# Three low halves of the first two experts' weights on GpSimd, and the next experts' loads reordered

## The chip, the cores and the metric

The kernel runs on one core of a Trainium2 chip. A core has five engines that run at the same time and meet only through semaphores: TensorE (PE) multiplies matrices, VectorE (DVE), ScalarE (ACT) and GpSimd (POOL) work on elements, and SyncE (SP) issues transfers. Sixteen DMA engines move data between the main memory and the on-chip memory SBUF; PE writes to PSUM. The metric is the device time of one execution in microseconds (us), less is better.

## The reference, cut to what matters

One layer of a diffusion backbone over 640 tokens (128 of a prompt, 512 of a latent grid), model width 1024. After attention, convolution, output projection and LayerNorm comes a mixture of 16 experts. Each token picks one group of four experts and two experts in it:

```
g_idx = top_k(softmax(t @ wg + bg), 1);  e_idx = top_k(softmax(logits of that group), 2)
hid = t @ w_exp_in[e]            # 1024 x 512 for each expert
a, up = split(hid)
y   = (silu(a) * up * gate) @ w_exp_out[e]     # 256 x 1024
x   = layer_norm(ALPHA * x + gf * sum over the two experts of y)
```

All data are fp32.

## The kernel before, in words

**Precision.** Every fp32 matrix is split into a high part, rounded to the type fp32r (by ACT, a copy), and a low part, the rest (a subtraction by DVE). A product is three matmuls: high x high, high x low, low x high (lines 1756 to 1758). So each weight half that arrives in `raw` needs an ACT copy to `w_hi` and then a subtraction `w_lo = raw - w_hi` before PE may use it, and its home in `raw` is free for the next load when `w_lo` is there.

**Names.** The input weights of expert e come in two halves of 1 MB, h = 0 and 1. The prediction writes in(e,h) for the load of such a half (`expert_in`, line 514), out(e) for the load of the output weights (`expert_out`, line 526), w_hi(e,h) for the ACT copy (`expert_whi`, line 953) and half (e,h) or low half (e,h) for the subtraction (`expert_wlo`, line 1424; for (0,1) before the change `first_wlo_quarter`, line 1433). There are two homes for input weights and two for output weights; expert e uses home e mod 2. `olo` (line 1499) is the subtraction for the output weights, `act_lo` (line 1521) that of the activations.

**Stages.** The attention ends at about 280 us. Then, for five tiles of 128 tokens in turn, PE computes the output projection, DVE the LayerNorm (lines 1440 to 1497), the modulated rows h2, and, some tiles behind, the choice of experts from the router's logits (`choose`, line 1381) and the token's place in the expert's list with one-hot comparisons (`put`, line 1409). POOL stores each tile of h2 to main memory (line 651), from where each expert's rows are gathered by an indirect DMA (line 657). The rows of expert 0 aren't gathered from memory: PE picks them with one-hot products out of SBUF (`gather_first`, line 2077), the last of them when the last tile's places are known. Then the expert loop begins: for each expert an up projection in two halves (line 2152), transposes of the next expert's rows (line 2138), and the down projection of the expert before (line 2170).

**What sets the order.** Each engine's instructions stand in the program in a fixed order, and semaphores hold them. On DVE the tail of the last tile is followed by the choices and places of the last two tiles (lines 1526 to 1529), the low halves of expert 0, the list of places (line 1540), the low halves of expert 1, and the loop (line 1647). On SP the loads stand in one queue; each waits until its home is free, and one that waits holds all behind it. `s_wlo` counts the low halves with h = 0, `s_wlp` those with h = 1. in(1,1) and out(0) also wait for the last tile's h2, because their homes hold data of the LayerNorm until then. POOL has nothing to do beside DMAs in this stretch: the stores of h2, then, once the list is ready, the gathers and the stores of expert rows.

Of the kernel before, what the change touches and what calls it, by code (L numbers as in the profile page):

```python
# [5 lines left out]
def build(nc, ins, outs):  # L6


    fp32 = mybir.dt.float32
# [3 lines left out]
    ALU = mybir.AluOpType  # L13
# [10 lines left out]
    NT = TOK // P  # L24
# [10 lines left out]
    NE = ins["w_expert_in"].shape[1]  # L35
# [3 lines left out]
    CH = 512  # L39
# [33 lines left out]
    with ctx:  # L73
        def sb(name, shape, dt=fp32):
            return ctx.enter_context(nc.sbuf_tensor(name, shape, dt))

        def sem(name):
            return ctx.enter_context(nc.semaphore(name))
# [4 lines left out]
        w_hi = sb("w_hi", [P, 2, KD * CH], fp32r)  # L83
        w_lo = sb("w_lo", [P, 2, KD * CH], fp32r)
        raw = sb("raw", [P, 2, KD * CH])
# [30 lines left out]
        def dap(t, offset, pattern):  # L116
            return bass.AP(tensor=t.tensor, offset=offset, ap=pattern)
# [125 lines left out]
        E0 = 2 * NW  # L243
# [22 lines left out]
        s_whi = sem("w_hi_ready")  # L266
        s_wlo = sem("w_lo_ready")
        s_wlp = sem("expert_w_lo_second_half_ready")
        s_whp = sem("expert_w_hi_second_half_ready")
# [121 lines left out]
        def raw_slot(b):  # L391
            return raw[:, b, :].rearrange("p (k n) -> p k n", k=KD)
# [38 lines left out]
        def out_rows(t):  # L431
            return outs["y_prompt"][0] if t == NT - 1 else outs["y_sample"][0][t * P:(t + 1) * P, :]
# [3 lines left out]
        def _(sp):  # L436
# [77 lines left out]
            def expert_in(e, h):  # L514
                slot = e % 2
                if h == 0 or e < 2:
                    sp.wait_ge(s_wlo, e + E0 - 1)
                else:
                    sp.wait_ge(s_wlp, e - 1)
                if e == 1:  # L520

                    sp.wait_ge(s_h2, 1 if h == 0 else H2)
                src = we_in[e].rearrange("(k p) n -> p k n" if e == 0 else "(p k) n -> p k n", p=P)
                sp.dma_start(raw_slot(slot)[:, 4 * h:4 * h + 4, :], src[:, 4 * h:4 * h + 4, :]).then_inc(s_raw[slot][h], 16)

            def expert_out(e):
                slot = e % 2
                if e < 2:

                    sp.wait_ge(s_h2, H2)  # L530
                    sp.wait_ge(s_h2t, NT)
                    sp.wait_ge(s_h2s[2 * e], 16)
                    if e == 1:
                        sp.wait_ge(s_h2s[1], 16)
                        sp.wait_ge(s_hgt, 1)
                else:
                    sp.wait_ge(s_olo, e - 1)
                sp.dma_start(raw_o[:, slot, :].rearrange("p (k n) -> p k n", k=2),
                             we_out[e].rearrange("(p k) n -> p k n", p=P)).then_inc(s_rawo[slot], 16)
# [3 lines left out]
            for t in T_ORDER[:-1]:  # L543
                sp.dma_start(out_rows(t), dap(ins["ln2_b"], 0, [[0, P], [1, D]])).then_inc(s_pre, 16)
            expert_in(1, 0)
            expert_in(1, 1)
            expert_out(0)
            expert_in(2, 0)
            for e in range(2, NE + 2):

                if 2 < e < NE:
                    expert_in(e, 0)
                if e >= 4:
                    expert_out(e - 2)
                if e < NE:
                    expert_in(e, 1)
                if e == 2:
                    expert_out(1)

            sp.wait_ge(s_wlo, E0 + NE - 1)  # L560
            sp.wait_ge(s_wlp, NE - 1)
# [31 lines left out]
        def _(pool):  # L593
# [36 lines left out]
            def load_bias(g, a, last_use):  # L630

                if g >= 1:
                    pool.wait_ge(s_nm, 2 * (NB * (g - 1) + last_use) + 2)
                for side in range(2):
                    src = dap(bias_dram, (2 * g + side) * CB * 3 * TW + a * TW,
                              [[SPAN, ROWS], [3 * TW, CB], [1, LOC]])
                    pool.dma_start(bias_s[:, side, a, :], src).then_inc(s_bias[a], 16)  # L637
# [6 lines left out]
            for g in range(HP):  # L644
                load_bias(g, 2, 0)
                load_bias(g, 1, 2)
                load_bias(g, 0, 3)
            for n, t in enumerate(T_ORDER):

                pool.wait_ge(s_h2, n + 1 if n < NT - 1 else H2)  # L650
                pool.dma_start(h2_dram[t * P:(t + 1) * P, :].rearrange("p (k c) -> p k c", k=KD), h2_held[n]).then_inc(s_h2s[n], 16)
            pool.wait_ge(s_lc, 1)
            for n in range(NT):
                pool.wait_ge(s_h2s[n], 16)
# [56 lines left out]
        def _(act):  # L711
# [205 lines left out]
            def h2_copy(n):  # L917
                act.wait_ge(s_h2t, n + 1)
                if n >= 1:
                    act.wait_ge(s_lg, n)  # L920
                else:
                    act.wait_ge(s_mlo, HP + 1)
                for i in range(2):
                    if n == NT - 1:
                        act.wait_ge(s_h2t, NT + i)
                    nc.scalar.activation(h2_T[:, 4 * i:4 * i + 4, :], PS[:, 4 + i, :].rearrange("p (k t) -> p k t", k=4),
                                         ACT.Copy).then_inc(s_h2c, 1)

            def logits_copy(n):

                act.wait_ge(s_lp, n + 1)
                nc.scalar.activation(group_logits, PS[:, 4, 0:P], ACT.Copy).then_inc(s_lcp, 1)

            def root(n):

                act.wait_ge(s_var, n + 1)
                nc.scalar.activation(std[:, n % 2:n % 2 + 1], mv[:, n % 2, 1:2], ACT.Sqrt, bias=eps).then_inc(s_std, 1)
# [15 lines left out]
            def expert_whi(e, h):  # L953

                b = e % 2
                if e == 0:
                    act.wait_ge(s_mo0, 1)
                elif e == 1:
                    act.wait_ge(s_mo, NT)
                else:  # L960
                    act.wait_ge(s_hid, e - 1)
                act.wait_ge(s_raw[b][h], 16 * (len(LOADS[b]) + e // 2 + 1))
                half = slice(h * 4 * CH, (h + 1) * 4 * CH)
                nc.scalar.activation(w_hi[:, b, half], raw[:, b, half], ACT.Copy).then_inc((s_whi, s_whp)[h], 1)  # L964
# [41 lines left out]
                nc.scalar.activation(y_sb[:, 1, CH:D], PS[:, 3, :], ACT.Copy).then_inc(s_ya, 1)  # L1006

            expert_whi(0, 0)
            h2_copy(NT - 2)
            root(NT - 1)  # L1010
            logits_copy(NT - 2)
            expert_whi(0, 1)
            h2_copy(NT - 1)
            logits_copy(NT - 1)

            expert_whi(1, 0)
            expert_whi(1, 1)
            for h in range(2):
                if h == 0:
# [39 lines left out]
            with act.If(more > 0):  # L1059
# [3 lines left out]
                with act.Fori(0, more) as i:  # L1063

                    e = act.value_load(over_i[0:1, bass.ds(i + 1, 1)], min_val=0, max_val=NE - 1)
# [67 lines left out]
        def _(dve):  # L1133
# [8 lines left out]
            V = nc.vector  # L1142
# [281 lines left out]
            def expert_wlo(e, b, h):  # L1424
                if h == 0:
                    dve.wait_ge(s_whi, e + E0 + 1)
                else:
                    dve.wait_ge(s_whp, e + 1)
                half = slice(h * 4 * CH, (h + 1) * 4 * CH)
                V.tensor_tensor(w_lo[:, b, half], raw[:, b, half], w_hi[:, b, half].bitcast(fp32),  # L1430
                                ALU.subtract).then_inc((s_wlo, s_wlp)[h], 1)

            def first_wlo_quarter(k):

                dve.wait_ge(s_whp, 1)
                quarter = slice(k * CH, (k + 2) * CH)
                return V.tensor_tensor(w_lo[:, 0, quarter], raw[:, 0, quarter], w_hi[:, 0, quarter].bitcast(fp32), ALU.subtract)

            link(V.memset(uni[:, 5120:5200], 0.0))
            for n, t in enumerate(T_ORDER):  # L1440
# [58 lines left out]
            def expert_olo(e, b):  # L1499
                dve.wait_ge(s_ohi, e + 1)  # L1500
                oh, ol = {NE - 1: wo_last, NE - 2: wo_near}.get(e, (wo_hi, wo_lo)) if isinstance(e, int) else (wo_hi, wo_lo)
                V.tensor_tensor(ol, raw_o[:, b, :].rearrange("p (k n) -> p k n", k=2), oh.bitcast(fp32),  # L1502
                                ALU.subtract).then_inc(s_olo, 1)

            def gathered_lo(c, b):
                dve.wait_ge(s_ghi, c)
                V.tensor_tensor(hgT_lo[:, b, :, :], PS[:, 2:4, :].rearrange("p a (k t) -> p (a k) t", k=4),
                                hgT_hi[:, b, :, :].bitcast(fp32), ALU.subtract).then_inc(s_glo, 1)
# [24 lines left out]
            d12 = rs[:, 160:160 + NT]  # L1533
            link(V.tensor_tensor(gexp, logits[:, :, 0:NG], g_top[:, :, 0:1].to_broadcast([P, NT, NG]), ALU.subtract))
            V.tensor_tensor(d12, e_top[:, :, 1], e_top[:, :, 0], ALU.subtract).then_inc(s_d12, 1)
            expert_wlo(0, 0, 0)
            first_wlo_quarter(4)
            dve.wait_ge(s_ls, NT)
            second = list_t[:, 0:NE]
            link(V.tensor_scalar(second, PS[:, 7, 0:NE], PAGE - AWAY, -float(PAGE), ALU.is_ge, ALU.mult))  # L1540
# [11 lines left out]
                V.tensor_scalar(list_last[:, h:h + 1], PS[:, 7, NE - 1:NE], 2.0, 2.0 * AWAY + h, ALU.mult, ALU.add)  # L1552
            V.tensor_scalar(list_d[:, 0:NE], PS[:, 7, 0:NE], AWAY, None, ALU.add).then_inc(s_lc, 1)
            dve.wait_ge(s_gi, 1)
            first_wlo_quarter(6).then_inc(s_wlp, 1)
            expert_olo(0, 0)
            silu_times_up(0, 0)
            act_lo_sub(0, 0)
            gathered_lo(1, 1)
            expert_wlo(1, 1, 0)  # L1560
            expert_wlo(1, 1, 1)

            def chunk_count():

# [741 lines left out]
```

## Time and profile before

| | |
|---|---|
| median of three runs | 566.56 us |
| lowest and highest run | 565.86 and 571.65 us |
| the profiled execution: its span, first to last instruction | 567.2 us |
| PE busy | 510.6 us, 90% |
| DVE busy | 443.0 us, 78% |
| ACT busy | 272.9 us, 48% |
| POOL busy | 106.2 us, 19% |
| main memory, over the span | 257 GB/s |

The profile is that of one execution. It has no time of its own beside its span, which is 0.6 us above the median of the runs. Instructions are told by engine, source line and operation; "idle before" is how long the engine stood before an instruction, with what released it behind the arrow. The ends of matmuls are modelled, so their durations overlap: a row of 0.39 us stands for about 0.23 us of PE's time.

### The profile page before, as it was taken

The page shows a single profiled execution, that of the slowest core. Times are in us where ns is not written, and L with a number is a line of the kernel's source. Part 1 is how long each engine was busy: PE and PEld are TensorE (multiplying, and loading weights), DVE is VectorE, ACT ScalarE, POOL GpSimd, SP SyncE. Part 2 cuts the span into 40 slices and gives each one's busy share as a digit, 9 for nine tenths or more (in the row PEclk, how much of TensorE's full clock was granted, in tenths as well). Part 3 has the DMA queues.
Part 4 walks back from the last instruction along what each step waited for, and adds up shares of the span by engine and source line. Part 5 has one row for each costly group of instructions (what it writes and reads, how often), then busy time and mean ns, then how long its engine had stood idle before and what let it go on. Part 6 is the DMA issues. An engine that isn't in the chain of part 4 may idle for free.

```text
span 567.2 us, 8067 instructions
## 1 busy us (share of the span) xinstructions
PE 510.6 (90%) x3120; PEld 419.6 (74%) x3120; DVE 443.0 (78%) x720; ACT 272.9 (48%) x378; POOL 106.2 (19%) x114
## 2 busy tenths in 40 slices
PE   4899999999999998789999998989999999999670
PEld 1569999987889995566787887867887777777220
DVE  3216999989699407998479878789988989887895
ACT  2327402021312217787612225368888787794363
POOL 0005700021000002220000000214433354212301
PEclk9999999999999999999999999899999999999786
DMA  8997995639686712229097114589999999968577
GB/s 299 387 386 231 252 354 164 222 98 322 218 292 221 200 25 57 53 54 250 24 368 277 48 50 153 196 305 412 398 398 367 375 371 373 381 250 309 207 239 158
DMA packets 55743, 138.17 MB, mean 244 GB/s; under 512 B 8311, under 2 KB 17074, under 8 KB 49816
## 3 DMA queue, kind: packets, MB, share of 16 engines
q1 hardware_dynamic: 43704, 114.87, 57.0%
q0 software_dynamic: 9120, 20.80, 12.6%
q10 hardware_dynamic: 2880, 1.98, 1.2%
q8 instruction: 25, 0.41, 0.3%
q14 instruction: 14, 0.11, 0.1%
HBM read 127.61 MB, written 18.10 MB: 257 GB/s over the span
## 4 chain that ended last, share of the span: by engine, by line
PE 40%; DVE 25%; DMA 19%; issue 8%; ACT 5%; SPq 1%; POOL 0%; DVEq 0%; POOLq 0%; ACTq 0%
DMA uni<-in_w_expert_out 14%; PE PS L1854 7%; PE PS L1855 7%; PE PS L1859 7%; DVE uni L1195 4%; PE PS L1756 3%; DVE act_lo L1502 3%; PE PS L1758 3%; PE PS L1757 3%; DMA uni<-in_w_ada 2%; DMA raw<-in_w_ada 2%; PE PS L2237 2%; ACT act_hi L974 2%; DVE w_lo L1430 2%; DVE PS L1305 1%
## 5 line engine op out<-in xcount | busy, mean ns | idle before, releaser
L1756 PE MATMUL PS<-w_hi,act_hi 128*128 128x512 f32 x256 | 103.7, 405 | 2.4 <-DVE act_lo L1523 0.9
L1758 PE MATMUL PS<-w_hi,act_lo 128*128 128x512 f32 x256 | 100.1, 391 | 0.0
L1757 PE MATMUL PS<-w_lo,act_hi 128*128 128x512 f32 x256 | 99.9, 390 | 0.0
L1854 PE MATMUL PS<-act_hi,w_hi 128*128 128x320 f32 x320 | 97.5, 313 | 2.2 <-issue 1.5
L1855 PE MATMUL PS<-act_lo,w_hi 128*128 128x320 f32 x320 | 96.3, 309 | 0.0
L1195 DVE SCALAR_TENSOR_TENSOR uni<-raw,uni 128x512 f32<-128x512 f32 x112 | 75.3, 748 | 0.5 <-DMA raw<-in_w_ada 0.4
L1859 PE MATMUL PS<-act_hi,w_lo 128*128 128x320 f32 x320 | 72.9, 309 | 0.0
L1430 DVE TENSOR_TENSOR w_lo<-raw,w_hi 128x2048 fp32r<-128x2048 f32 x31 | 70.7, 2285 | 0.7 <-ACT w_hi L964 0.6
L964 ACT ACTIVATE w_hi<-raw 128x2048 fp32r<-128x2048 f32 x32 | 61.3, 1916 | 16.6 <-DMA raw<-in_w_expert_in 13.6
L1854 PEld LDWEIGHTS PS<-act_hi,w_hi 128*128 128x128 f32 x320 | 60.1, 188 | 5.2 <-issue 4.2
L1855 PEld LDWEIGHTS PS<-act_lo,w_hi 128*128 128x128 f32 x320 | 60.1, 188 | 0.0
L1756 PEld LDWEIGHTS PS<-w_hi,act_hi 128*128 128x128 f32 x256 | 48.1, 188 | 14.5 <-issue 2.9
L1758 PEld LDWEIGHTS PS<-w_hi,act_lo 128*128 128x128 f32 x256 | 48.1, 188 | 10.6
L1757 PEld LDWEIGHTS PS<-w_lo,act_hi 128*128 128x128 f32 x256 | 48.2, 188 | 8.8
L724 ACT ACTIVATE w_hi<-raw 128x2048 fp32r<-128x2048 f32 x14 | 26.3, 1916 | 57.9 <-PE PS L1859 50.4
L1859 PEld LDWEIGHTS PS<-act_hi,w_lo 128*128 128x128 f32 x320 | 53.5, 188 | 0.0
L664 POOL DMA_INDIRECT expert_rows<-uni,cols x15 | 26.4, 1763 | 87.3 <-ACT uni L998 87.3
L1502 DVE TENSOR_TENSOR act_lo<-uni,act_hi 128x2048 fp32r<-128x2048 f32 x14 | 32.1, 2291 | 11.6 <-ACT act_hi L974 11.6
L637 POOL DMA_DIRECT2D uni<-bias_windows x24 | 15.7, 664 | 116.1 <-DVE small L1305 115.6
L657 POOL DMA_INDIRECT uni<-h_rows,cols x15 | 30.4, 2028 | 32.6 <-PE PS L2087 14.0
L1161 DVE TENSOR_TENSOR w_lo<-raw,w_hi 128x2048 fp32r<-128x2048 f32 x14 | 31.6, 2288 | 5.2 <-ACT w_hi L724 5.2
L1305 DVE CUSTOM_DVE_ANT_1 PS<-PS,uni 128x512 f32<-128x512 f32 x32 | 21.5, 713 | 16.5 <-issue 15.7
(270 smaller groups left out, 853.6 us busy)
## 6 DMA issues: line engine op xcount, KB each, us to landing
raw<-in_w_expert_in SPq DMA_DIRECT2D x32, 1024.0 KB, 15.0
raw<-in_w_ada SPq DMA_DIRECT2D x20, 1024.0 KB, 7.9
uni<-in_w_expert_out SPq DMA_DIRECT2D x16, 1024.0 KB, 15.7
raw<-in_w_in SPq DMA_DIRECT2D x12, 1024.0 KB, 7.9
uni<-expert_rows SPq DMA_DIRECT2D x10, 512.0 KB, 7.4
uni<-in_w_ada SPq DMA_DIRECT2D x4, 1024.0 KB, 14.5
raw<-in_w_out SPq DMA_DIRECT2D x4, 1024.0 KB, 6.0
uni<-bias_windows POOLq DMA_DIRECT2D x24, 128.0 KB, 3.3
```

Of the source, the lines that this page charges most:

```text
L657: pool.indirect_dma_start(hg[:, b, :], None, h2_dram, bass.IndirectOffsetOnAxis(ap=col, axis=0), bounds_check=TOK - 1, oob_is_err=False).t ...
L964: nc.scalar.activation(w_hi[:, b, half], raw[:, b, half], ACT.Copy).then_inc((s_whi, s_whp)[h], 1)
L1161: V.tensor_tensor(w_lo[:, i % 2, half], raw[:, SLOT["w", i], half], w_hi[:, i % 2, half].bitcast(fp32), ALU.subtract).then_inc(s_wlo, 1)
L1195: V.scalar_tensor_tensor(out=acc, in0=w, scalar=cond[:, k, j:j + 1], in1=acc, op0=ALU.mult, op1=ALU.add).then_inc(s_adl, 1)
L1430: V.tensor_tensor(w_lo[:, b, half], raw[:, b, half], w_hi[:, b, half].bitcast(fp32), ALU.subtract).then_inc((s_wlo, s_wlp)[h], 1)
L1502: V.tensor_tensor(ol, raw_o[:, b, :].rearrange("p (k n) -> p k n", k=2), oh.bitcast(fp32), ALU.subtract).then_inc(s_olo, 1)
L1756: T.matmul(out, lh, rh, start=first, stop=False)
L1757: T.matmul(out, lh, rl, start=False, stop=False)
L1758: return T.matmul(out, ll, rh, start=False, stop=last)
L1854: T.matmul(out, a, h_hi[:, k, sl], start=f, stop=False)
L1855: T.matmul(out, a, h_lo[:, k, sl], start=False, stop=False)
L1859: mm = T.matmul(out, b, h_hi[:, k, sl], start=False, stop=l)
```

## The change

GpSimd gets a function `early_wlo` and runs it for (0,0) ahead of its last store of h2, and for (0,1) and (1,0) behind it. DVE keeps (1,1), which it now does where it did (0,0), and loses the others. ACT makes w_hi(0,1) directly behind w_hi(0,0), and w_hi(1,0) where it made w_hi(0,1). SP's order was in(1,0), in(1,1), out(0), in(2,0), in(2,1), out(1), in(3,0), in(3,1), in(4,0), out(2), in(4,1); it becomes in(1,0), in(2,0), in(1,1), out(0), in(2,1), in(3,0), in(3,1), out(1), out(2), in(4,0), in(4,1). Two waits are added on DVE so that it keeps the order of the two counters.

```
 SP:
             expert_in(1, 0)
+            expert_in(2, 0)
             expert_in(1, 1)
             expert_out(0)
-            expert_in(2, 0)
-            for e in range(2, NE + 2):
-
-                if 2 < e < NE:
+            expert_in(2, 1)
+            expert_in(3, 0)
+            expert_in(3, 1)
+            expert_out(1)
+            expert_out(2)
+            for e in range(4, NE + 2):
+
+                if e < NE:
                     expert_in(e, 0)
-                if e >= 4:
+                if e >= 5:
                     expert_out(e - 2)
                 if e < NE:
                     expert_in(e, 1)
-                if e == 2:
-                    expert_out(1)
 GpSimd:
+            def early_wlo(e, h):
+
+                if h == 0:
+                    pool.wait_ge(s_whi, e + E0 + 1)
+                else:
+                    pool.wait_ge(s_whp, e + 1)
+                half = slice(h * 4 * CH, (h + 1) * 4 * CH)
+                nc.gpsimd.tensor_tensor(w_lo[:, e, half], raw[:, e, half], w_hi[:, e, half].bitcast(fp32),
+                                        ALU.subtract).then_inc((s_wlo, s_wlp)[h], 1)
+
             for n, t in enumerate(T_ORDER):
 
+                if n == NT - 1:
+                    early_wlo(0, 0)
                 pool.wait_ge(s_h2, n + 1 if n < NT - 1 else H2)
                 pool.dma_start(h2_dram[t * P:(t + 1) * P, :]...
+            early_wlo(0, 1)
+            early_wlo(1, 0)
             pool.wait_ge(s_lc, 1)
 ScalarE:
             expert_whi(0, 0)
+            expert_whi(0, 1)
             h2_copy(NT - 2)
             root(NT - 1)
             logits_copy(NT - 2)
-            expert_whi(0, 1)
+            expert_whi(1, 0)
             h2_copy(NT - 1)
             logits_copy(NT - 1)
 
-            expert_whi(1, 0)
             expert_whi(1, 1)
 VectorE:
             def expert_wlo(e, b, h):
                 if h == 0:
                     dve.wait_ge(s_whi, e + E0 + 1)
+                    if isinstance(e, int) and e == 2:
+                        dve.wait_ge(s_wlo, E0 + 2)
                 else:
                     dve.wait_ge(s_whp, e + 1)
+                    if isinstance(e, int) and e == 1:
+                        dve.wait_ge(s_wlp, 1)
...
-            expert_wlo(0, 0, 0)
-            first_wlo_quarter(4)
+            expert_wlo(1, 1, 1)
             dve.wait_ge(s_ls, NT)
...
             dve.wait_ge(s_gi, 1)
-            first_wlo_quarter(6).then_inc(s_wlp, 1)
             expert_olo(0, 0)
             silu_times_up(0, 0)
             act_lo_sub(0, 0)
             gathered_lo(1, 1)
-            expert_wlo(1, 1, 0)
-            expert_wlo(1, 1, 1)
```

## Rows read from the trace of the kernel before

**Rows 1.** Stages: width, busy us of PE, PEld, DVE, ACT, POOL; clock, DMA share, GB/s.
```profile
355.00:357.50 2.50, 2.50 (x15) 2.50 (x16) 2.36 (x7) 0.24 (x1) 0.00 (x0) 0.62 0.47 193
398.00:500.00 102.00, 97.01 (x466) 78.98 (x464) 90.51 (x72) 82.10 (x71) 39.16 (x20) 1.00 0.98 377
```

**Rows 2.** Chain that ended last, in order of time: start us, us, what.
```profile
354.89 4.57 PE PS L2087 x24
...
417.48 16.47 DMA uni<-in_w_expert_out
...
458.41 16.22 DMA uni<-in_w_expert_out
...
500.15 0.50 PE PS L1756
...
509.79 0.40 PE PS L1756
```

**Rows 3.** DVE in order of time, last tile and choices: start us, us, instruction, idle before.
```profile
338.82 0.69 DVE L1470 SCALAR_TENSOR_TENSOR uni<-g,uni 128x512 f32<-128x512 f32 x1
...
340.58 0.43 DVE L1417 TENSOR_TENSOR uni<-const,cols 128x256 f32<-128x256 f32 x1
...
348.69 0.18 DVE L1392 TENSOR_TENSOR uni<-uni,logits 128x16 f32<-128x16 f32 x1
...
349.60 0.19 DVE L1396 TENSOR_TENSOR uni<-const,cols 128x32 f32<-128x32 f32 x1
...
350.57 0.18 DVE L1387 TENSOR_TENSOR logits<-PS,rb 128x24 f32<-128x24 f32 x1 [0.26 <-PE PS L2075]
```

**Rows 4.** PE in order of time: first matmul of four projections.
```profile
361.42 0.50 PE L1756 MATMUL PS<-w_hi,act_hi 128*128 128x512 f32 x1
...
365.06 0.47 PE L1756 MATMUL PS<-w_hi,act_hi 128*128 128x512 f32 x1 [0.58 <-DVE w_lo L1437]
...
374.81 0.50 PE L1756 MATMUL PS<-w_hi,act_hi 128*128 128x512 f32 x1 [0.90 <-DVE w_lo L1430]
...
389.58 0.50 PE L1756 MATMUL PS<-act_hi 128*128 128x512 f32 x1 [0.66 <-DVE act_lo L1523]
```

**Rows 5.** DVE in order of time: low halves of the first experts.
```profile
356.54 2.29 DVE L1430 TENSOR_TENSOR w_lo<-raw,w_hi 128x2048 fp32r<-128x2048 f32 x1
...
372.47 6.68 DVE L1430 TENSOR_TENSOR w_lo<-raw,w_hi 128x2048 fp32r<-128x2048 f32 x3
```

**Rows 6.** ACT in order of time: w_hi(0,0), a copy of h2, w_hi(0,1).
```profile
334.77 1.92 ACT L964 ACTIVATE w_hi<-raw 128x2048 fp32r<-128x2048 f32 x1 [2.96 <-PE PS L1758]
341.99 1.09 ACT L926 ACTIVATE uni<-PS 128x512 f32<-128x512 f32 x2 [5.30 <-PE PS L2057]
...
344.99 1.90 ACT L964 ACTIVATE w_hi<-raw 128x2048 fp32r<-128x2048 f32 x1
```

**Rows 7.** SP's queue in order of time: start us, us, load issued.
```profile
374.78 4.73 SPq L524 DMA_DIRECT2D raw<-in_w_expert_in  x3
379.56 0.43 SPq L538 DMA_DIRECT2D uni<-in_w_expert_out  x1
383.95 3.32 SPq L524 DMA_DIRECT2D raw<-in_w_expert_in  x2
```

**Rows 8.** POOL's memsets by shape: count, busy us, mean ns.
```profile
L597 POOL MEMSET wr<- 128x256 f32 x1 | 0.3, 311 | 0.0
L594 POOL MEMSET rows<- 128x128 f32 x1 | 0.2, 204 | 0.3 <-POOLq L2293 0.3
```

**Rows 9.** POOL in order of time, and one DVE operation beside it.
```profile
338.48 0.53 POOL L651 DMA_DIRECT2D h_rows<-uni  x1 [13.23 <-DVE uni L1494]
347.93 0.53 POOL L651 DMA_DIRECT2D h_rows<-uni  x1 [8.92 <-DVE uni L1494]
...
425.49 2.29 DVE L1502 TENSOR_TENSOR act_lo<-uni,act_hi 128x2048 fp32r<-128x2048 f32 x1 [1.27 <-ACT act_hi L974]
...
425.58 3.09 POOL L657 DMA_INDIRECT uni<-h_rows,cols  x1 [0.50 <-issue]
...
435.81 1.01 POOL L657 DMA_INDIRECT uni<-h_rows,cols  x1 [0.37 <-issue]
```

More of the change, by code:

```diff
@@ L1431, in expert_wlo @@
                                 ALU.subtract).then_inc((s_wlo, s_wlp)[h], 1)
[L1433 to L1437, printed above, removed]
             link(V.memset(uni[:, 5120:5200], 0.0))
```

## The prediction

> **What bounds the kernel now.** I read the stages first, then the chain of waits, then the instructions around the seam between the output projection and the expert loop. From 398 to 500 us the DMA engines are busy 98% of the time, and VectorE (DVE) 89% [rows 1]; the chain there runs from one load of an expert's output weights to the next, 417.48 to 458.41 for four experts, 10.2 us each [rows 2]. So for most of the expert loop the weight stream sets the pace, and an engine that is freed there gives nothing. The end can only come earlier by what the stream gains before it is saturated, around 375 to 380 us, or later by what delays its seam. TensorE (PE) is not far behind: from its down projection of expert 12 (500.15) to the next, behind the last loads, is 9.6 us by the chain [rows 2].
>
> Ahead of the loop the chain runs through DVE: the last tile's LayerNorm and its choice of experts, up to the 24 one-hot gather products at 354.89 [rows 2]. Those rows have no slack: one small operation follows the other, and between the end of one tile's choice and the logits of the last one DVE waits only 0.26 us [rows 3]. That is where GpSimd's new work is put.
>
> **What is removed.** DVE loses three halves: (0,0), (0,1) and (1,0). The first, at 356.54, and half of the second lie under the gather products, which end only where the first up projection begins, 361.42: they are worth nothing. The last quarter held PE for 0.58 us at 365.06, and (1,0) held it for 0.90 at 374.81 [rows 4, 5]. Both waits go. From 372.47 DVE has three halves of 2.29 us back to back, 6.68 us [rows 5]; two go (one entirely, (1,1) moves ahead to 356.5, where DVE then waits for the placement list anyway). Behind them DVE is full up to the act_lo of expert 1, for which PE waits at 389.58 [rows 4]. What is late next is the ACT copy of the gathered rows and of w_hi: followed through, the up projection of expert 1 begins about 1.7 us earlier and the down projection of expert 1 1.6 us earlier.
>
> **What is moved.** ACT's w_hi(0,1) goes ahead of a copy that ACT waits for anyway (idle from 336.7 to 341.99); w_hi(1,0) takes the place where w_hi(0,1) stood [rows 6]. Cost zero; without that gap it would be 1.9 us. In SP's queue in(2,0) is put ahead of in(1,1). It waits for the low half (0,0), due at about 344, and in(1,1) waits until 347.7 for h2: it doesn't get late while GpSimd takes under 8 us. out(2) goes ahead of in(4,0); its own wait (olo of expert 0, about 366) is over long before in(4,0) is due.
>
> **What the stream gains.** Between 355 and 377 the DMA engines have holes. Today in(3,0), in(3,1), in(4,0) and out(2) are all issued from 374.78 to 379.56 [rows 7]. At the 377 GB/s of the saturated stream [rows 1] a load of 1 MB takes 2.8 us, and the rows gathered and stored for an expert 1.9 us together. By 382.2 the four loads and a gather are 12.2 us of work, of which at most 7.4 are done: 4.8 us are in arrears. With the change in(2,0), in(2,1), in(3,0), in(3,1), out(1), out(2) are issued as their homes come free, ahead of expert 1's up projection, and in(4,0) at the end of the low half (2,0), about 375.4; all are down by 378. in(4,1) then follows 1.7 us before today's 383.95 [rows 7], at 382.2, with nothing in arrears. The lead is 4.8 us, less a hole of about 0.8 while the queue has nothing but in(4,1), until in(5,0) follows: **4.0 us**. It can't grow, because the two homes of each kind are full. From there arrivals (10.2 us of work in the 9.6 that PE needs) keep the stream busy. Bounds: 1.6, if only the shift of the consumer counts, and 6.1, if PE at 9.6 us per expert were the bound (388.0 + 11 x 9.6 = 494.0 against 500.15 [rows 2]).
>
> **What GpSimd's three halves cost.** No row has a two-input operation on GpSimd. GpSimd's memset takes 107 ns for 128 further elements, 0.84 ns for one access [rows 8]. Two reads in turn make 2048 x 1.67 = 3.4 us, two reads and a write in turn 5.1 us; DVE's 2.29 us [rows 5] is the lower end. I take 4.3, the middle of the two by memset, since no row says whether the write takes a turn. The time of its own is covered: GpSimd has no other work between its stores of h2 and the first gather.
>
> What isn't covered is the interface that GpSimd reads through. An indirect DMA on GpSimd takes 0.99 us alone. Where it starts in a DVE operation with two SBUF inputs, it lasts until 0.88 us behind that one's end: it starts at 425.58, the DVE operation ends at 427.78, it ends at 428.67. The one at 435.81, 0.11 us ahead of such an operation, takes 1.01 us [rows 9]. Ten further pairs agree to 0.1 us. So in this trace GpSimd's read waits for a whole DVE instruction; it isn't shared element by element. How DVE fares while GpSimd reads for long, no row shows: those DMAs read one column. Bounds: nothing, or the rest of the GpSimd instruction. By symmetry I take the second. The Trainium skill has it so too ("SBUF — State Buffer", Who interferes with whom: an exclusive lock on the shared interface against a DVE instruction with two SBUF inputs, the one that starts first holding it for its whole instruction); no run here shows that side. Its "GPSIMD Engine Reference", section 3.1, gives 4497 ns for this shape: an estimate by it has 11.6 in place of the 11.0 below.
>
> With a duration T, on today's times:
> - (0,0) gets in behind the DVE operation that ends at 339.5, and ends at 339.5 + T. The next DVE operation with two SBUF inputs, the one-hot comparison, is due at 340.58 [rows 3]: T - 1.1.
> - (0,1) follows the last store of h2 (issued 347.93, 0.53 us [rows 9]), from 348.5. The next such DVE operation is due at 348.69 [rows 3]: T - 0.1.
> - (1,0) follows at once; the choice runs up to its comparison, 0.9 us further on [rows 3], and is held for T - 0.7.
>
> Together 3T - 1.9 = **11.0 us** (5.0 with T = 2.3, 13.4 with T = 5.1); the 0.26 us of slack I leave aside. PE's clock adds a little at most: while it waited ahead of 354.89 the granted clock fell, 0.62 from 355 to 357.5 [rows 1], and the 24 products took 4.57 us; a second such spell is 1.5 us at most, and I count none.
>
> The loop and its stream move with the first up projection, since every home comes free by the consumers. Sum: 567.2 + 11.0 - 4.0 = 574.2 against the profiled span of 567.2; the median of the runs is 566.56, 0.6 lower. **Forecast 573.6 us.**
>
> **Rivals.**
> 1. **GpSimd's reads don't hold DVE**, or only for single accesses. Then the seam stays at 361.4 and only the lead is left: 566.6 - 4.0 = **562.6**, not slower. For it: nothing in this trace shows DVE held, and its 2048-element operations spread over 12 ns with GpSimd busy beside them. Against it: GpSimd itself is held for whole instructions. It turns at a hold of 4.0 us in all, 1.3 us per GpSimd instruction. Chance 0.27.
> 2. **The stream isn't the bound but its latency is**: then the gain is up to 6.1 and not 4.0. With holds 571.5, without them **560.5**. Against it: 98% DMA share over 102 us [rows 1]. Chance 0.06.
> 3. **GpSimd is much slower** than memset says, as with a rounding of the output to fp32r: at T = 7, 19 us of holds and in(1,1) late: **582**. Chance 0.07.
> 4. **The change doesn't run early**: GpSimd's first half needs w_hi(0,0), which ends at 336.7 [rows 6], ahead of the store at 338.48 [rows 9], so it can hardly be held up; then nothing changes but the removed waits, 565. Chance 0.02.
>
> **How the numbers follow.** The forecast's case has 0.58. Its own range is 567.6 (T = 2.3) to 576.0 (T = 5.1), and a point either way for the lead. About 1% (5.7 us) is what a measurement tells from no change, so faster is below 560.9 and slower above 572.2. In the forecast's case slower has 0.45 (T over 3.9) and same 0.13; rival 1 has 0.24 same and 0.03 faster; rival 2 shares 0.03 faster, 0.03 same; rival 3 is slower; rival 4 same. Faster 0.06, same 0.42, slower 0.52. To leave out no more than 2 in 10 the range goes from 562.0, with most of rival 1, to 577.5.
>
> **What would show it.** GpSimd rows of about 4.3 us for w_lo from about 339.5, 352 and 356.5. Right: DVE's one-hot comparison within the last tile's LayerNorm starts some 3 us behind the operation before it, the choices of the last two tiles are drawn out by about 8 us, and the first up projection begins near 372. Wrong, by rival 1: it begins at 361 and no DVE gap stands beside a GpSimd row. The lead: in(2,0) is issued at about 344, in(3,0) ahead of the first up projection's end, nothing in arrears when in(4,0) is issued, and the distance from the first up projection to the down projection of expert 12 shrinks from 138.7 to about 135 us. If it shrinks by 6 or by 1.6, the term of the lead is what was wrong.

## The result, and the profile after

The changed kernel takes 579.69 us in the median of four runs (577.75 to 580.77), the kernel before 566.21 on the same occasions: ratio 1.0226, 95% interval 1.0188 to 1.0264. It is 13.5 us slower. The forecast was slower, by 7; the time lies 2.2 us above the range.

The profiled execution has a span of 578.2 us, 11.0 more than before. DVE in order of time (start us, us, instruction, idle before), from the changed kernel; its lines 1485, 1434, 1408, 1409 and 1404 answer to 1470, 1417, 1391, 1392 and 1387 of [rows 3]:

```profile
338.38 5.43 DVE L1485 SCALAR_TENSOR_TENSOR uni<-g,uni 128x512 f32<-128x512 f32 x1
...
344.89 0.42 DVE L1434 TENSOR_TENSOR uni<-const,cols 128x256 f32<-128x256 f32 x1
...
352.74 9.13 DVE L1408 TENSOR_SCALAR uni<-const,cols 128x16 f32<-128x16 f32 x1
361.91 0.18 DVE L1409 TENSOR_TENSOR uni<-uni,logits 128x16 f32<-128x16 f32 x1
...
363.44 0.17 DVE L1404 TENSOR_TENSOR logits<-PS,rb 128x24 f32<-128x24 f32 x1
...
369.39 2.29 DVE L1451 TENSOR_TENSOR w_lo<-raw,w_hi 128x2048 fp32r<-128x2048 f32 x1
```

GpSimd in order of time:

```profile
338.04 0.53 POOL L666 DMA_DIRECT2D h_rows<-uni  x1 [13.23 <-DVE uni L1509]
338.68 4.58 POOL L658 TENSOR_TENSOR w_lo<-raw,w_hi 128x2048 fp32r<-128x2048 f32 x1
352.24 0.57 POOL L666 DMA_DIRECT2D h_rows<-uni  x1 [8.98 <-DVE uni L1509]
352.83 9.00 POOL L658 TENSOR_TENSOR w_lo<-raw,w_hi 128x2048 fp32r<-128x2048 f32 x2
```

Of the kernel before, the second of these operations (L1391) and a cast that an experiment below turns on:

```profile
348.43 0.23 DVE L1391 TENSOR_SCALAR uni<-const,cols 128x16 f32<-128x16 f32 x1
...
349.40 0.17 DVE L1395 CAST cols<-cols 128x2 f32<-128x2 uint32 x1
```

The reader is to see two long DVE rows beside the two GpSimd rows (the second is of two instructions). Before, the first lasted 0.69 us [rows 3] and the second 0.23. There is no gap ahead of them: a held instruction shows as a long one, not as idle time. They are 4.74 and 8.90 us longer, 13.64 in all, and both stand on the chain that ended last.

PE in order of time; the answers to [rows 2, 4]:

```profile
367.75 5.49 PE L2098 MATMUL PS<-uni 128*128 128x128 f32 x24 [0.55 <-DVE uni L1438]
...
375.23 0.50 PE L1767 MATMUL PS<-w_hi,act_hi 128*128 128x512 f32 x1
...
382.32 1.16 PE L2160 MATMUL PS<-const,uni 128*128 128x128 f32 x8 [1.32 <-DMA uni<-h_rows,cols]
...
402.12 0.50 PE L1767 MATMUL PS<-act_hi 128*128 128x512 f32 x1 [0.66 <-DVE act_lo L1538]
...
509.98 0.50 PE L1767 MATMUL PS<-act_hi 128*128 128x512 f32 x1 [0.79 <-DVE act_lo L1538]
```

Stages (columns as in [rows 1]), and SP's queue as in [rows 7]:

```profile
350.00:352.50 2.50, 1.86 (x9) 1.89 (x10) 2.40 (x7) 1.21 (x2) 0.26 (x1) 0.50 0.00 0
352.00:362.00 10.00, 8.24 (x49) 7.35 (x48) 9.83 (x7) 3.23 (x4) 9.57 (x3) 0.50 0.91 335
420.00:512.00 92.00, 88.72 (x430) 73.24 (x429) 83.53 (x67) 75.52 (x66) 30.07 (x18) 1.00 0.97 375
```

```profile
343.29 9.06 SPq L524 DMA_DIRECT2D raw<-in_w_expert_in  x2
352.45 0.37 SPq L538 DMA_DIRECT2D uni<-in_w_expert_out  x1
357.38 14.66 SPq L524 DMA_DIRECT2D raw<-in_w_expert_in  x3
375.38 5.09 SPq L538 DMA_DIRECT2D uni<-in_w_expert_out  x2
389.21 10.60 SPq L524 DMA_DIRECT2D raw<-in_w_expert_in  x3
```

**Two distances** make traces comparable, because an execution's stages ahead of the seam end up to 2.8 us apart in the eleven traces (the fourth store of h2 starts between 338.03 and 340.82). The seam is the distance from that store to the first up projection: 361.42 - 338.48 = 22.94 before, 375.23 - 338.04 = 37.19 after, **14.25 more**. The loop is the distance from the first up projection to the down projection of expert 12: 138.73 before, 509.98 - 375.23 = 134.75 after, **3.98 less**. With the start of the seam 0.44 earlier and the last stages, 68.2 against 67.05, 1.17 longer, that is the 11.0. The last stages spread from 65.7 to 68.2 in the traces at hand, so the 1.17 isn't told from chance. The seam repeats well: 37.19 in both kernels that have the three subtractions and differ in the loads alone, and 22.94 or 22.50 in the four traces with nothing new ahead of the first up projection, that of before among them.

**The trace of before is of a long execution.** In every execution with both figures on record the time is 1.8 to 2.2 us above the span. The spans of the kernel before have medians of 564.9, 565.0 and 564.9 us in the three sets of runs beside the experiments (17, 23 and 17 executions), and the traced one has 567.2, 2.2 to 2.3 more. The trace of the changed kernel, 578.2, is 0.55 above its median. So what a trace says against that of before is to be held against the medians: here the seam is 14.25 longer and the medians differ by 13.5. That leaves 0.8 us that the loop and the ends gained (-0.7 to 3.6 by the interval of the ratio), where the traces say 3.25 (14.25 less 11.0).

### The profile page after: what moved, and what is told of

Its sections match the earlier page's. It is cut to its first block, busy times and chain, and to the rows that moved or that the text cites. A ratio compares the mean times of both kernels' runs of the same rounds, so it can differ in the third digit from the quotient of the medians.

```text
span 578.2 us, 8070 instructions
## 1 busy us (share of the span) xinstructions
PE 516.6 (89%) x3120; PEld 425.3 (74%) x3120; DVE 449.9 (78%) x716; ACT 272.8 (47%) x378; POOL 114.7 (20%) x117
## 4 chain that ended last, share of the span: by engine, by line
PE 50%; DVE 21%; DMA 14%; issue 8%; ACT 4%; SPq 1%; POOL 0%; POOLq 0%; DVEq 0%; ACTq 0%
DMA uni<-in_w_expert_out 8%; PE PS L1865 8%; PE PS L1866 7%; PE PS L1870 7%; PE PS L1767 6%; PE PS L1769 6%; PE PS L1768 6%; DVE act_lo L1517 2%; DMA uni<-in_w_ada 2%; DVE uni L1408 2%; DVE uni L1485 1%; DVE PS L1322 1%; ACT act_hi L991 1%; DMA uni<-expert_rows 1%; DVE w_lo L1451 1%
## 5 line engine op out<-in xcount | busy, mean ns | idle before, releaser
L1451 DVE TENSOR_TENSOR w_lo<-raw,w_hi 128x2048 fp32r<-128x2048 f32 x29 | 66.3, 2286 | 1.7 <-ACT w_hi L981 1.2
L1178 DVE TENSOR_TENSOR w_lo<-raw,w_hi 128x2048 fp32r<-128x2048 f32 x14 | 31.6, 2286 | 6.2 <-ACT w_hi L741 6.2
L674 POOL DMA_INDIRECT uni<-h_rows,cols x15 | 24.5, 1633 | 34.3 <-PE PS L2160 16.7
## 6 DMA issues: line engine op xcount, KB each, us to landing
raw<-in_w_expert_in SPq DMA_DIRECT2D x32, 1024.0 KB, 13.3
uni<-in_w_expert_out SPq DMA_DIRECT2D x16, 1024.0 KB, 12.1
```

Of the source, the lines that this page charges most:

```text
L1178: V.tensor_tensor(w_lo[:, i % 2, half], raw[:, SLOT["w", i], half], w_hi[:, i % 2, half].bitcast(fp32), ALU.subtract).then_inc(s_wlo, 1)
```

## The experiments

Except where a size is given, an experiment is told by seam and loop of its trace, beside the ratio of its runs to runs of the kernel before on the same chip.

**What holds DVE: reads or any GpSimd instruction.** GpSimd's subtraction replaced by a memset:

```
-                nc.gpsimd.tensor_tensor(w_lo[:, e, half], raw[:, e, half], w_hi[:, e, half].bitcast(fp32),
-                                        ALU.subtract).then_inc((s_wlo, s_wlp)[h], 1)
+                nc.gpsimd.memset(w_lo[:, e, half].bitcast(fp32), 0.0).then_inc((s_wlo, s_wlp)[h], 1)
```

> The changed kernel, with each of GpSimd's three subtractions replaced by one memset of the same low half: GpSimd writes 2048 elements (1.8 us by the memset rows) and reads nothing. Left out: those three low halves are zero and not the remainders. Theory A (VectorE is held by GpSimd's read of its SBUF operands): the two drawn-out VectorE operations (5.43 and 9.13 us) go back to 0.69 and 0.23 us, the first up projection begins at about 361, the lead of 4 us stays: 562 us, ratio 0.993. Rival B (every GpSimd instruction on SBUF holds VectorE): they take 2.2 and 3.8 us, the seam is 5 us late: 567 to 568. Mixed case (only the tensor_scalar, which can write through both port pairs, is held by a write): 0.69 and 3.8 us, 565 to 566.

Measured: 568.64 us against 566.85, ratio 1.0026 (1.0003 to 1.0048). GpSimd and DVE in order of time:

```profile
340.67 1.83 POOL L658 MEMSET w_lo<- 128x2048 f32 x1
...
350.12 3.56 POOL L658 MEMSET w_lo<- 128x2048 f32 x2
```

```profile
340.49 0.69 DVE L1484 SCALAR_TENSOR_TENSOR uni<-g,uni 128x512 f32<-128x512 f32 x1
...
350.10 3.62 DVE L1407 TENSOR_SCALAR uni<-const,cols 128x16 f32<-128x16 f32 x1
```

The operation with two SBUF operands is free beside a write (0.69), the tensor_scalar is not: 3.62 against 0.23. It is the mixed case. The seam is 4.0 us longer (first up projection at 367.10), which is the 3.39 of the hold and 0.92 of slow clock (24 products 5.49 us, 4.57 before), less the slack; the loop is 134.09, 4.6 less. The trace balances to a gain of 0.6; the runs say a loss of 1.8, more than the forecast of 565 to 566. The difference is the trace of before: its span is 2.2 above the median of its runs, while this kernel's trace, 566.9, is at the median. By the medians the loop and the ends gained 2.2 us (1.3 to 3.8) and not 4.6.

**One input instead of two.** The subtraction replaced by a copy:

```
+                nc.gpsimd.tensor_copy(w_lo[:, e, half], raw[:, e, half]).then_inc((s_wlo, s_wlp)[h], 1)
```

> The changed kernel, with each of GpSimd's three subtractions replaced by a copy of the raw half into the low half: one read instead of two. Left out: the subtraction, so those low halves hold the whole weight. Theory A (the hold lasts as long as the reading instruction, whatever its number of inputs): GpSimd's rows shorten to 1.8 to 3.4 us and the two VectorE operations to that much plus 0.7 and twice that plus 0.2. Rival (it takes two inputs on both engines to collide): no hold, 0.69 and 0.23 us.

```profile
340.66 1.91 POOL L658 CAST w_lo<-raw 128x2048 fp32r<-128x2048 f32 x1
...
352.07 3.73 POOL L658 CAST w_lo<-raw 128x2048 fp32r<-128x2048 f32 x2
```

```profile
340.48 2.65 DVE L1484 SCALAR_TENSOR_TENSOR uni<-g,uni 128x512 f32<-128x512 f32 x1
...
352.04 3.80 DVE L1407 TENSOR_SCALAR uni<-const,cols 128x16 f32<-128x16 f32 x1
```

One read is enough: the DVE operation takes 0.69 + 1.96, and the hold follows the length of the GpSimd instruction (1.91). The copy is as short as the memset, so it isn't the length but the read that makes the difference between 0.69 and 2.65. 572.11 us in one run. Theory A holds.

**Are two GpSimd instructions one hold?** GpSimd waits for its own result between (0,1) and (1,0):

```
             early_wlo(0, 1)
+            pool.wait_ge(s_wlp, 1)
             early_wlo(1, 0)
```

> The changed kernel, with GpSimd waiting for the completion of (0,1) before it starts (1,0). Theory A (two GpSimd instructions in a row keep the interface, because the second is already queued when the first ends): the pause of 0.1 us or more lets VectorE's waiting tensor_scalar through after 4.6 us, and a later two-operand or tensor_scalar operation of the choice is held for another 4 us; two rows of 4 to 5 us in place of one of 9.13. Rival (the held instruction has to wait until GpSimd has nothing more, or GpSimd wins each time): one row of 9.1 to 9.3 us again. The time is the same within noise in both, 578 to 581.

```profile
354.31 4.67 DVE L1409 TENSOR_SCALAR uni<-const,cols 128x16 f32<-128x16 f32 x1
...
359.71 3.87 DVE L1413 CAST cols<-cols 128x2 f32<-128x2 uint32 x1
```

```profile
359.01 4.55 POOL L658 TENSOR_TENSOR w_lo<-raw,w_hi 128x2048 fp32r<-128x2048 f32 x1
```

DVE gets in, once: theory A. Back to back, the second instruction keeps the interface. What is held next is a cast of two elements (0.17 us before), not the comparison with two operands right behind it. Seam 13.6 longer, loop 133.9; 577.96 in one run.

**One hold alone.** Only (0,0) on GpSimd:

```
             expert_in(1, 0)
+            expert_in(2, 0)
             expert_in(1, 1)
             expert_out(0)
-            expert_in(2, 0)
...
-            early_wlo(0, 1)
-            early_wlo(1, 0)
...
-            expert_wlo(1, 1, 1)
+            expert_wlo(0, 0, 1)
...
             gathered_lo(1, 1)
+            expert_wlo(1, 1, 0)
+            expert_wlo(1, 1, 1)
```

(The SyncE part is against the kernel before, the rest against the changed one.)

> Only (0,0) is on GpSimd, ahead of its last store of h2; (0,1), (1,0) and (1,1) are on VectorE; loads as before, but in(2,0) ahead of in(1,1). Theory A (each hold is paid in full, and once, by the seam): one hold of 4.7 us, no second one; the first up projection begins 4.5 to 5 us later, the lead is 1 to 2 us (in(2,0) early, the 0.58 us wait gone): 569 to 570 us, ratio 1.006. Rival (the holds cost less than they last, because something else is late anyway; the damage is by the pair behind the last store or by the slow clock): 566 to 567.

Measured: 571.45 us, ratio 1.0079 (1.0057 to 1.0102), 1.5 above the forecast, and the seam says why. The traced execution is the longest of the four (574.22). DVE, PE and stages of this kernel:

```profile
338.69 5.43 DVE L1480 SCALAR_TENSOR_TENSOR uni<-g,uni 128x512 f32<-128x512 f32 x1
...
357.41 0.18 DVE L1399 TENSOR_TENSOR logits<-PS,rb 128x24 f32<-128x24 f32 x1 [2.48 <-PE PS L2083]
...
361.06 0.17 DVE L1414 TENSOR_TENSOR uni<-uni 128x16 f32<-128x16 f32 x1 [1.40 <-PE PS L2105]
```

```profile
350.94 1.09 PE L2065 MATMUL PS<-const,uni 128*128 128x128 f32 x4 [1.37 <-DVE uni L1504]
...
357.20 3.40 PE L2095 MATMUL PS<-uni 128*128 128x128 f32 x16
...
369.61 0.50 PE L1764 MATMUL PS<-w_hi,act_hi 128*128 128x512 f32 x1
```

```profile
350.00:352.50 2.50, 1.56 (x8) 1.59 (x9) 2.40 (x6) 1.27 (x2) 0.00 (x0) 0.50 0.00 0
357.50:360.00 2.50, 2.50 (x13) 2.50 (x13) 1.85 (x12) 1.91 (x1) 0.00 (x0) 0.50 1.00 416
```

The hold is 4.74, but the seam is 8.3 longer (369.61 - 338.35). While DVE is held PE runs out of work, and the granted clock falls to 0.50, the lower of its two levels, by 350. Then the last tile's transposes, router and gather products run slowly (16 gather products in 3.40 us; such a group took 1.95 or 2.03 before), and DVE waits 2.48 us for the last logits where it waited 0.26 [rows 3], and 1.40 behind those 16 products where it didn't wait. These 3.6 us are the rest of the 8.3: the price of the slow clock, indirectly. Theory A is right about the hold and wrong in that the seam pays the hold alone. In the changed kernel this is mostly hidden, since the second hold lies over it; 0.92 us at the last 24 products is left.

**The halves without the load order**, the changed kernel with SyncE's order of before:

```
-            expert_in(2, 0)
             expert_in(1, 1)
             expert_out(0)
-            expert_in(2, 1)
-            expert_in(3, 0)
-            expert_in(3, 1)
-            expert_out(1)
-            expert_out(2)
...
+            expert_in(2, 0)
+            for e in range(2, NE + 2):
```

> GpSimd's three halves and the changed VectorE and ScalarE order as in the changed kernel, but SyncE's load order as before. The hold stays (13.6 us at the same place), the first up projection begins at about 375 us. Theory A (the lead of 4.0 us from the first up projection to the down projection of expert 12 comes from both parts together: homes come free earlier by the halves, and the order lets the loads follow): the old order has in(2,0) behind in(1,1) and out(0), and in(3,0) behind out(1), which waits for the last gather product; the lead shrinks to 2 to 3 us, time 581 to 582. Rival B (the order gives nothing, the early halves all): lead 4.0, time 579.7 as with the change. Rival C (the order gives all): lead 0 to 1, time 583 to 584.

Measured: 585.1 us, ratio 1.0316 (1.0287 to 1.0345). PE in order of time:

```profile
377.38 0.50 PE L1764 MATMUL PS<-w_hi,act_hi 128*128 128x512 f32 x1
...
387.40 1.97 PE L2157 MATMUL PS<-const,uni 128*128 128x128 f32 x8 [4.29 <-DMA uni<-h_rows,cols]
...
517.62 0.50 PE L1764 MATMUL PS<-act_hi 128*128 128x512 f32 x1 [0.66 <-DVE act_lo L1535]
```

The seam is 37.19, the same as after. The loop is 140.24: nothing is gained, 1.5 us are lost. None of the three theories had that. out(1), in(3,0) and in(3,1) are now issued at 377.5 to 379, together with the gather of expert 1's rows, and PE waits 4.29 us for those rows. The order is worth 5.5 us of the loop, given the halves; the medians of the two kernels, 585.1 and 579.69, differ by 5.4.

**The load order without the halves**, the kernel before with SyncE's new order alone; its edit is the SyncE part of the change's diff:

> The kernel before with SyncE's new load order alone; the low halves stay on VectorE where they were. Theory A: the homes come free no earlier, so nothing can be issued earlier; out(1) even moves back from 365 to 377 us, behind in(3,1), and is needed at 385: time as before, 566 to 568, ratio 1.00. Rival C (the order gives all of the lead): 562 to 563.

Measured: 578.82 us, ratio 1.0216 (1.0187 to 1.0245). I had overlooked the head of the queue. SyncE and PE:

```profile
358.40 0.82 SPq L524 DMA_DIRECT2D raw<-in_w_expert_in  x2
359.33 0.36 SPq L538 DMA_DIRECT2D uni<-in_w_expert_out  x1
```

```profile
369.77 0.80 PE L1759 MATMUL PS<-w_hi,act_hi 128*128 128x512 f32 x1 [10.37 <-DVE act_lo L1552]
```

in(2,0) waits for the low half (0,0), which is DVE's and ends at 358.4. in(1,1) and out(0), due at 347.7, stand behind it until then. ScalarE waits for in(1,1) ahead of its copy of expert 0's rows, and PE 10.37 us for that. The seam is 8.8 us longer (369.77 - 338.03 = 31.74) and the loop as before (138.9); the runs differ by 12.1, and both traced executions are away from their medians. So this kernel measures another fault and not the order's worth: the order needs the early half (0,0).

**A place where the read costs nothing.** The kernel before, with (1,0) on GpSimd behind its gather for expert 2:

```
                     if c == 1:
                         nc.gpsimd.memset(small[:, 102:103], 0.0).then_inc(s_gi, 1)
+                    if c == 2:
+                        pool.wait_ge(s_whi, E0 + 2)
+                        nc.gpsimd.tensor_tensor(w_lo[:, 1, 0:4 * CH], raw[:, 1, 0:4 * CH], w_hi[:, 1, 0:4 * CH].bitcast(fp32),
+                                                ALU.subtract).then_inc(s_wlo, 1)
...
+                    if isinstance(e, int) and e == 2:
+                        dve.wait_ge(s_wlo, E0 + 2)
...
             gathered_lo(1, 1)
-            expert_wlo(1, 1, 0)
```

> The kernel before with one half only, (1,0), on GpSimd, put behind its gather for expert 2, where VectorE has no operation that reads two SBUF operands until 372.5 us; all else as before. Theory A (the hold needs an operation of VectorE that uses the shared interface at that time): GpSimd's subtraction waits for the low half of the output weights (ends 367.1) and runs 367.1 to 371.7; no VectorE operation is drawn out; TensorE's 0.90 us wait ahead of expert 1 goes, the home comes free 3 us earlier, VectorE has 2.3 us less; the gain is 1 to 3 us, time 563.5 to 565.5, ratio 0.995 to 0.998. Rival B (GpSimd holds VectorE whatever it does): the two silu operations of 0.42 us or the 0.42 us act_lo are drawn out to 3 to 4 us and the down projection of expert 0 is late: 568 to 570.

> The kernel with (1,0) alone on GpSimd behind its gather for expert 2, once more, to have its gain over the kernel before from a second set of runs. Theory: the distance from the first up projection to the down projection of expert 12 is 133.8 us against 138.7, of which the runs' times show 2 to 5: ratio 0.993 to 0.998. Rival: the first set's gain was the spread of the stages ahead: ratio 1.000.

Measured: 564.62 us, ratio 0.9966 (0.9941 to 0.9991), and again 564.68, ratio 0.9970 (0.9935 to 1.0004). Of the first set GpSimd, DVE, PE:

```profile
366.16 5.58 POOL L682 TENSOR_TENSOR w_lo<-raw,w_hi 128x2048 fp32r<-128x2048 f32 x1
```

```profile
365.05 2.28 DVE L1508 TENSOR_TENSOR act_lo<-uni,act_hi 128x2048 fp32r<-128x2048 f32 x1
368.75 0.42 DVE L1519 SCALAR_TENSOR_TENSOR uni<-uni,PS 128x256 f32<-128x256 f32 x1 [1.41 <-ACT uni L989]
...
370.63 0.42 DVE L1529 TENSOR_TENSOR act_lo<-PS,act_hi 128x256 fp32r<-128x256 f32 x1 [1.01 <-ACT act_hi L993]
371.55 1.23 DVE L1513 TENSOR_TENSOR act_lo<-PS,act_hi 128x1024 fp32r<-128x1024 f32 x1 [0.49 <-ACT act_hi L984]
372.69 4.48 DVE L1436 TENSOR_TENSOR w_lo<-raw,w_hi 128x2048 fp32r<-128x2048 f32 x2
```

```profile
362.52 0.50 PE L1761 MATMUL PS<-w_hi,act_hi 128*128 128x512 f32 x1 [1.13 <-DVE act_lo L1555]
...
496.32 0.50 PE L1761 MATMUL PS<-act_hi 128*128 128x512 f32 x1 [0.61 <-DVE act_lo L1529]
```

Now it is GpSimd's row that is long: it waits for the DVE operation that ends at 367.33 and works 4.4 us behind it. Under it DVE's operations read one operand from PSUM, and none is drawn out. The seam is no longer than before (22.50), the loop is 133.80, and in the second set's trace 22.50 and 133.43. Against the trace of before that is 4.9 us less in the loop; the runs give 2.1 and 2.0 in all, since that trace is long. Against the traces of the changed kernel and of its variants with a memset or a pause (134.75, 134.09, 133.90) the loop is no longer: one half, rightly placed, gives as much there as three halves and a new order did, without their seam. Theory A, and the fastest kernel of the study, by 0.3%; the second set's interval reaches to 1.0004.

**The same, with out(2) ahead of in(3,0):**

```
+            expert_in(2, 1)
+            expert_out(1)
+            expert_out(2)
+            for e in range(3, NE + 2):
```

> The kernel with (1,0) alone on GpSimd behind its gather for expert 2, with out(2) issued ahead of in(3,0): its home is free at 367.3, when the DMA engines still have holes. Theory A (the load stream is the bound behind the seam, each hole closed is gained): holes of 0.3 to 0.6 us between 365 and 375 can be filled: 0 to 1 us less than with that half alone, 563.5 to 564.7. Rival: the load takes bandwidth from in(3,0) and the gathered rows, and gives nothing: 564.6 or up to 1 us more.

Measured: 566.6 us, ratio 0.9997 (0.9969 to 1.0026). The loop is 499.74 - 363.76 = 135.98, 2.2 longer than without the step, and the medians differ by 2.0:

```profile
391.58 0.50 PE L1762 MATMUL PS<-act_hi 128*128 128x512 f32 x1 [1.53 <-DVE act_lo L1530]
```

The rival holds: PE waits 1.53 us ahead of the down projection of expert 1, where it waited 0.65.

## Why the prediction was right in its direction and wrong in its size

**What bounds, and the lead.** What bounds is right: the stream is at a DMA share of 0.97 from 420 to 512 us. The lead's size is right between the two traces only: the loop lost 3.98 us where 4.0 were forecast. That match is likely luck in part, because the traced execution of before is 2.2 to 2.3 us longer than the median. By the medians the loop and the ends gained 0.8 us in this kernel and 2.2 in the one with memsets, nearer to the lower bound of 1.6. With one trace of before, how much of its excess lies in the loop stays open. The path to the lead is another in part: expert 1's rows land late and PE waits 1.32 us for them, behind out(1) and out(2); so the down projection of expert 1 is 1.3 us nearer to the first up projection and not 1.6 (26.89 against 28.16). Rival 2, a gain of up to 6.1, is out. The removed waits of 0.58 and 0.90 us are gone, as forecast.

**The holds, the step that failed.** The mechanism was right, against rival 1: DVE is held for the rest of each of the three GpSimd instructions, on the chain. The sum, 3T - 1.9 = 11.0, was mis-sized; it measured 13.64, and 13.3 on the seam, with the slack taken off. It was also added up wrong: its rows give T - 0.2 for (0,1) (348.5 to 348.69) and T - 0.9 for (1,0), so 3T - 2.2 = 10.7. Three parts, told from the sum as it stands:
- T is 4.5 to 4.6 us, not 4.3. That alone would have made 11.6.
- (0,0) was to get in behind the DVE operation that starts at 338.8 and hold only the comparison. It held that operation itself, whose row (338.38 after the change) starts 0.30 us before GpSimd's: 4.74 in place of 3.4. The same 5.43 us stands in all four kernels with this subtraction at this place.
- (0,1) and (1,0) were to let DVE run 0.8 us between them, up to the next operation with two SBUF operands. But a tensor_scalar with one operand in SBUF is held as well, and DVE gets in only if GpSimd pauses: 8.90 in place of 8.2. The pause run shows both.

**PE's clock.** "I count none" was wrong: 0.95 us at the last products and what follows in the changed kernel, and 3.6 us where only one hold lies before it. Its bound, 1.5, was exceeded in that run, because the slow stretch begins with the last tile's transposes and not with the gather.

**The sum.** By the traces the seam is 2.3 (holds) + 0.95 (clock) longer than forecast, the ends 0.7, the loop as forecast; that makes the trace's 11.0 of the expected 7.0. By the medians it is 13.5: the seam's 14.25 less 0.8. The 2.5 us between the two are the traced executions, a long one before and one near its median after. The forecast set the span of 567.2 beside the median of 566.56, which is a time, and read them as 0.6 us apart; a span of 567.2 is a time of about 569 (an estimate, by the 1.8 to 2.2 us between them), so its rows are those of an execution some 2.5 us longer than the median. By the medians the lead of 4.0 was then too large as well.

**The load order** was costed by one condition, that GpSimd takes under 8 us, and it held (in(2,0) issued at 343.3). That it would cost 12 us with a late half (0,0) was seen only in the order's run.

**The page's rule**, "SBUF — State Buffer" of the Trainium skill, section Who interferes with whom, is borne out on the side that the trace of before couldn't show: 0.69 becomes 5.43 beside a read, and stays 0.69 beside a write. Which of the two starts first can't be read from the starts of the profile's rows: the held DVE row starts 0.30 us ahead of GpSimd's, and in the kernel with (1,0) alone a DVE row that starts 1.11 us ahead holds GpSimd. It also counts copies, casts and tensor_scalar operations among those that can use both port pairs; the 9.13 us tensor_scalar and the 3.87 us cast agree, and so does the tensor_scalar held by a memset (3.62); the forecast had left them out. The figure of "GPSIMD Engine Reference", section 3.1, 4497 ns, agrees with 4.58 us better than my estimate from memsets did.

What stays open is how long the loop of the kernel before usually is, and with it the size of the lead: a second trace of that kernel would tell.

## What to carry to other kernels

Before elementwise work goes to GpSimd, list what VectorE does in exactly that stretch: an operation with two SBUF operands, and a cast or tensor_scalar in SBUF, was held here until the GpSimd instruction ended, and on a critical chain the hold is the price, however idle GpSimd was. Put the work where VectorE reads from PSUM or waits; there one half gained 2 us, and three on the chain lost 13.5. Before a trace's distances are trusted to a microsecond, see how its span stands to the median span of the runs. And a load put ahead of others in an in-order queue needs its home to be free earlier than theirs, by the engine that will really free it.

## What the runs showed of the hardware that I had not expected

- A held DVE instruction shows as a long row (9.13 us for 16 elements), not as idle time; its start can lie 0.30 us ahead of the GpSimd row that holds it.
- Two GpSimd instructions back to back hold once, for 9.0 us; with a semaphore wait between them VectorE gets in after 4.67.
- GpSimd's memset and its copy of 2048 elements take 1.83 and 1.91 us, its subtraction 4.58: a second input more than doubles the time.
- PE starved for 1.4 to 1.7 us at a time from 344 on, and its granted clock fell from 1.00 to 0.50 by 350. It stayed there for 10 us with one subtraction on GpSimd and for about 22 with all three.
